# Causal attention of the first block in three steps per pair of heads instead of four, and three orders in the grid attention

## The reference

```python
# fox: bias c[t]-c[s]; causal mask; 4 blocks of 128 queries over 512 keys
logits = q @ k.T * scale + cb[:, None] - cum_logf[None, :]
p = softmax(where(kpos <= qpos, logits, -inf)); o = p @ v
# diff: two softmaxes of 32-wide queries and keys
a = softmax(mask(q1 @ k1.T * s)) - lam * softmax(mask(q2 @ k2.T * s)); o = a @ v
# dsa: the top 128 causal keys by an index score
score = sum_h w[t,h] * relu(q_idx[t,h] @ k_idx[s]); sel = top_k(where(mask, score, -inf), 128)
o = softmax(where(selected & causal, q @ k.T * scale, -inf)) @ v
```

## Time and profile before

| | us |
|---|---|
| median of three runs | 2247.26 |
| profiled execution, its own time | 2243.46 |
| its span, first to last instruction | 2241.6 |
| TensorE matmuls busy | 2187.5 |
| VectorE busy | 1257.1 |
| ScalarE busy | 899.6 |
| GpSimd busy | 288.8 |

### The profile page before, as it was taken

The page is one execution under the profiler, slowest core; times in us unless marked ns, Lnnn a source line. Parts: engine busy times, 40 slices in busy tenths (PEclk is TensorE's granted clock), DMA queues, the critical chain, the costliest instruction groups (busy, mean ns, idle before and its releaser), DMA issues.

```text
span 2241.6 us, 31809 instructions
## 1 busy us (share of the span) xinstructions
PE 2187.5 (98%) x12938; PEld 1806.5 (81%) x12938; DVE 1257.1 (56%) x1750; ACT 899.6 (40%) x1574; POOL 288.8 (13%) x215
## 2 busy tenths in 40 slices
PE   7999999999999999999999999999999999999998
PEld 6876688888888876688888888989888887888777
DVE  5687648983224687548973226422666635212794
ACT  3447843222213447843222223232565524212673
POOL 3001322111222001322121000000010000000220
PEclk9999999999999999999999999999999999999999
DMA  5220016542553220015532321132000122311221
GB/s 164 89 71 2 1 60 204 187 133 85 139 174 97 89 71 1 1 64 199 190 129 85 127 105 53 56 97 76 15 23 9 52 76 96 129 58 57 72 72 57
DMA packets 136708, 194.20 MB, mean 87 GB/s; under 512 B 30789, under 2 KB 84050, under 8 KB 136562
## 3 DMA queue, kind: packets, MB, share of 16 engines
q1 hardware_dynamic: 110288, 169.83, 22.9%
q10 hardware_dynamic: 26114, 22.16, 3.5%
q0 software_dynamic: 160, 0.16, 0.0%
HBM read 180.46 MB, written 11.67 MB: 86 GB/s over the span
## 4 chain that ended last, share of the span: by engine, by line
PE 89%; DVE 5%; ACT 2%; issue 2%; ACTq 0%; DMA 0%; POOLq 0%; POOL 0%; DVEq 0%
PE ps L530 69%; PE ps L2740 3%; PE ps L1873 3%; PE ps L2757 2%; PE ps L2769 2%; DVE probs_t L2088 1%; PE ps L2286 1%; PE ps L2243 1%; PE ps L2272 1%; PE ps L2745 1%; PE ps L737 1%; PE ps L1907 1%; ACT probs_t L2846 1%; DVE neg_max L2055 1%; PE ps L537 1%
## 5 line engine op out<-in xcount | busy, mean ns | idle before, releaser
L495 DVE TENSOR_TENSOR w_low<-w_raw,w_high 128x2048 fp32r<-128x2048 f32 (+4 forms) x140 | 302.9, 2164 | 491.5 <-ACT w_high L490 491.3
L490 ACT ACTIVATE w_high<-w_raw 128x2048 fp32r<-128x2048 f32 (+4 forms) x140 | 252.9, 1807 | 602.0 <-PE ps L530 594.3
L530 PE MATMUL ps<-h_hi,w_high 128*128 128x512 f32 (+1 forms) x1168 | 439.5, 376 | 3.1 <-DVE w_low L495 1.8
L530 PE MATMUL ps<-h_lo,w_high 128*128 128x512 f32 (+1 forms) x1168 | 437.2, 374 | 0.0
L530 PE MATMUL ps<-h_hi,w_low 128*128 128x512 f32 (+1 forms) x1168 | 436.9, 374 | 0.0
L530 PEld LDWEIGHTS ps<-h_hi,w_high 128*128 128x128 f32 x1168 | 220.0, 188 | 44.1 <-DVE w_low L495 2.4
L530 PEld LDWEIGHTS ps<-h_hi,w_low 128*128 128x128 f32 x1168 | 219.8, 188 | 39.8
L530 PEld LDWEIGHTS ps<-h_lo,w_high 128*128 128x128 f32 x1168 | 220.0, 188 | 39.2 <-issue 0.5
L530 PE MATMUL ps<-w_high,h_hi 128*128 128x512 f32 (+3 forms) x576 | 214.2, 372 | 0.6 <-DVE h_lo L3142 0.6
L530 PE MATMUL ps<-w_low,h_hi 128*128 128x512 f32 (+3 forms) x576 | 211.6, 367 | 0.0
L530 PE MATMUL ps<-w_high,h_lo 128*128 128x512 f32 (+3 forms) x576 | 211.4, 367 | 0.0
(11 more groups left out here) (388 smaller groups left out, 3704.2 us busy)
## 6 DMA issues: line engine op xcount, KB each, us to landing
w_raw<-in_w_gate_up SPq DMA_DIRECT2D x44, 1024.0 KB, 5.1
ada_w<-in_ada_w SPq DMA_DIRECT2D x24, 1024.0 KB, 5.1
w_raw<-in_w_down SPq DMA_DIRECT2D x20, 1024.0 KB, 5.2
w_raw<-in_w_in SPq DMA_DIRECT2D x16, 1024.0 KB, 5.0
w_raw<-in_c_in_w SPq DMA_DIRECT2D x16, 1024.0 KB, 5.4
w_raw<-in_w_out SPq DMA_DIRECT2D x8, 1024.0 KB, 4.8
w_raw<-in_ab_in_w SPq DMA_DIRECT2D x8, 1024.0 KB, 5.1
masked_scratch<-mask_table ACTq DMA_DIRECT2D x8, 512.0 KB, 3.5
```

The lines of the kernel that those rows point to most:

```text
L490: e.activation(w_high[j % 2][:, 0:size], w_raw[j % 2][:, 0:size], ACT.Copy).then_inc(sig.w_high_done, 1)
L495: e.tensor_tensor(w_low[j % 2][:, 0:size], w_raw[j % 2][:, 0:size], w_high[j % 2][:, 0:size].bitcast(F32), ALU.subtract).then_inc(sig.w_lo ...
L530: mm = e.matmul(dst, lhs, rhs, start=start and a == 0, stop=stop and a == 2)
```

## The change

In `CausalPairs` a unit has three steps instead of four (`TILES = ((1,), (2, 0), (3,))`): query block 1 (two key blocks), query blocks 2 and 0 side by side in the same banks (3 + 1 key blocks), query block 3 (four). There are 30 steps. In the double step there are still two reductions and four exps, but one group of transposes, one copy and one group of `values`; its block 0 gets its mask (and gate) first and q times k last. `probs_ready` now counts halves, and `turn_probs` waits for each half on its own. The 37 top-k rounds are spread over the first 23 rounds of the loop, and the first dsa unit begins with step 21. On ScalarE `copy_o(u)` now stands in the round of the next unit's second step, between `copy_probs` and `exps`. The mask of block 0 lies beside that of block 2.

In `GridPairs` `values(s - 1)` now comes ahead of `wide`, and both high halves of pair 1 are made at s = -1.

```diff
@@ CausalPairs @@
-            ROUND_STEPS = 30
-            EARLY_PARTS = {32: 0, 33: 1, 36: 2}
+            TILES = ((1,), (2, 0), (3,))
+            PER = len(TILES)
+            ROUND_STEPS = 23
+            EARLY_PARTS = {24: 0, 25: 1, 27: 2}
...
-                self.steps = [(u, t) for u in range(len(self.units)) for t in range(NT)]
+                self.steps = [(u, tiles) for u in range(len(self.units)) for tiles in self.TILES]
...
+            def parts(self, s):
+
+                at_ = 0
+                for t in self.steps[s][1]:
+                    yield t, at_, (t + 1) * P
+                    at_ += (t + 1) * P
...
                 def scores(s):
...
-                    if x.kind == "dsa" and x.n == 0 and t:
-                        e.wait_ge(sig.keep_ready, B["keep_ready"] + t)
+                    if x.kind == "dsa" and x.n == 0:
+                        e.wait_ge(sig.keep_ready, B["keep_ready"] + max(tiles))
...
+                    first = parts[-1] if len(parts) == 2 else None
+                    if first:
+                        for m in range(2):
+                            added(*first, m, True, False)
+                            if x.kind == "fox":
+                                gated(*first, m, False)
+                    for t, a, w in reversed(parts):
+                        last = first and t == 0
+                        for m in range(2):
+                            e.matmul(ps[:, self.bank(s, m), a:a + w], q[x.rows(m), t * P:t * P + P], k[x.rows(m), 0:w], start=not last, stop=bool(last))
                     for m in range(2):
-                        e.matmul(ps[:, self.bank(s, m), 0:n], q[x.rows(m), t * P:n], k[x.rows(m), 0:n], start=True, stop=False)
...
+                        mm = added(*parts[0], m, False, True)
...
                 def turn_probs(s):
-                    u, t = self.steps[s]
-                    e.wait_ge(sig.probs_ready, B["probs_ready"] + s + 1)
                     for m in range(2):
-                        for kt in range(t + 1):
...
+                        e.wait_ge(sig.probs_ready, B["probs_ready"] + 2 * s + m + 1)
+                        for b in range(self.size(s) // P):
...
                     e.wait_ge(sig.turned_second, B["turned_second"] + s + 1)
-                    if t == 0 and u:
+                    if s % self.PER == 0 and u:
                         e.wait_ge(sig.o_done, B["o_done"] + u)
...
@@ CausalPairs.scalar @@
                     if 0 <= s < self.N:
                         copy_probs(s)
+                    if s > 1 and s % self.PER == 1:
+                        copy_o(s // self.PER - 1)
                     if s in self.mid:
                         copy_turned(self.mid[s])
                     if 0 <= s + self.AHEAD < self.N:
                         exps(s + self.AHEAD)
-                    if s >= NT and s % NT == 0:
-                        copy_o(s // NT - 1)
-                    if s % NT == 2 and s > 2 and self.units[s // NT - 1].kind == "diff":
-                        shift(s // NT - 1)
+                    if s % self.PER == 2 and s > 2 and self.units[s // self.PER - 1].kind == "diff":
+                        shift(s // self.PER - 1)
...
+                copy_o(self.U - 1)
@@ GridPairs @@
-                self.cut_at = {max(4 * p - 6, -1) + c: (p, c) for p in range(1, U) for c in range(2)}
+                self.cut_at = {-1: [(1, 0), (1, 1)]}
+                self.cut_at.update({4 * p - 6 + c: [(p, c)] for p in range(2, U) for c in range(2)})
...
                         self.scores(e, B, s + 2)
+                    if s >= 1:
+                        values(s - 1)
                     if s % 4 == 3:
                         wide(s // 4)
-                    if s >= 1:
-                        values(s - 1)
```

More of the change, by code:

```diff
@@ L1094, in vector @@
                         e.wait_ge(sig.parts_ready, B["parts_ready"] + 4)
[L1095 removed]
+                        ch.step(e.tensor_copy(keep_mask[:, 2, 3 * P:4 * P], cst("causal")[:, 384:512]))
                     if i == self.groups - 1:
@@ L2703, in final, with size, both @@
             def final(self, u):
-                return NT * u + NT - 1
+                return self.PER * (u + 1) - 1
             def bank(self, s, m):
                 return 2 * (s % self.SETS) + m
-            def both(self, s, n):
+            def parts(self, s):
[3 more added lines that the diff above has]
+                    at_ += (t + 1) * P
+            def size(self, s):
+                return sum((t + 1) * P for t in self.steps[s][1])
+            def both(self, s, a, n):
                 b = self.bank(s, 0)
-                return ps[:, b:b + 2, 0:n]
+                return ps[:, b:b + 2, a:a + n]
             def spare_bank(self, e, B, event):
@@ L2738, in scores, with added @@
                     q, k = q_turned[x.group % 2], kd_turned if x.kind == "dsa" else k_turned[x.group % 2]
-                    for m in range(2):
-                        e.matmul(ps[:, self.bank(s, m), 0:n], q[x.rows(m), t * P:n], k[x.rows(m), 0:n], start=True, stop=False)
[L2741 to L2745, removed]
+                    def added(t, a, w, m, start, stop):
+                        out_ = ps[:, self.bank(s, m), a:a + w]
+                        if x.kind == "dsa":
+                            at_ = a if t == 0 else 0
+                            mm = e.matmul(out_, ident_r[:], keep_mask[:, max(tiles), at_:at_ + w], start=start, stop=stop)
+                        else:
+                            mm = e.matmul(out_[:, w - P:w], ident_r[:], causal_r, start=start, stop=stop and x.kind != "fox")
+                        return mm
@@ new lines, in gated @@
+                    def gated(t, a, w, m, stop):
+                        h = 2 * x.n + m
+                        return e.matmul(ps[:, self.bank(s, m), a:a + w], gate_sel[:, h * P:(h + 1) * P], gate_t[:, 0:w], start=False, stop=stop)
+                    first = parts[-1] if len(parts) == 2 else None
[4 more added lines that the diff above has]
+                                gated(*first, m, False)
@@ L2749, in scores @@
-                            mm = e.matmul(ps[:, self.bank(s, m), 0:n], gate_sel[:, h * P:(h + 1) * P], gate_t[:, 0:n], start=False, stop=True)
+                            mm = gated(*parts[0], m, True)
                     mm.then_inc(sig.scores_ready, 1)
                 def turn_probs(s):
-                    u, t = self.steps[s]
-                    e.wait_ge(sig.probs_ready, B["probs_ready"] + s + 1)
                     for m in range(2):
-                        for kt in range(t + 1):
-                            mm = e.transpose(ps[:, self.bank(s, m), kt * P:(kt + 1) * P],
-                                             probs1[s % 3][:, m, kt * P:(kt + 1) * P], ident)
+                        e.wait_ge(sig.probs_ready, B["probs_ready"] + 2 * s + m + 1)
@@ L2832, in exps @@
                     for m in range(2):
-                        c = 2 * s + m
-                        ins = e.activation(probs1[s % 3][:, m, 0:n], ps[:, self.bank(s, m), 0:n], ACT.Exp,
-                                           bias=neg_max[:, c:c + 1], accum_out=sums[:, c:c + 1])
-                        if m == 0:
-                            ch.step(ins)
-                    ins.then_inc(sig.probs_ready, 1)
+                        for t, a, w in self.parts(s):
+                            c = 2 * NT * u + 2 * t + m
+                            ins = e.activation(probs1[s % 3][:, m, a:a + w], ps[:, self.bank(s, m), a:a + w], ACT.Exp,
+                                               bias=neg_max[:, c:c + 1], accum_out=sums[:, c:c + 1])
+                            if t != tiles[-1]:
+                                ch.step(ins)
+                        ins.then_inc(sig.probs_ready, 1)
                 def copy_probs(s):
-                    u, t = self.steps[s]
-                    n = (t + 1) * P
+                    n = self.size(s)
                     e.wait_ge(sig.probs_turned, B["probs_turned"] + s + 1)
```

55 lines of the change are left out of this document (30 added, 25 removed).

## The result

The changed kernel takes 2286.57 us, the median of four runs: 2281.28, 2283.96, 2289.18 and a disturbed one of 8192.17, which is in no ratio but lifts the median from 2283.96. The kernel before, run beside it on the same chip, takes 2245.88: a ratio of 1.0179 (95% interval 1.0165 to 1.0193), 1.8% slower. The forecast was 2262 with a range of 2249 to 2272: the sign was right, the size was not. The profiled execution took 2283.96 us with a span of 2282.2, so against the profiled execution of before 40.5 us are to be explained, where the sum of the prediction had 15.0.

A forecast was written before the change was run, and what follows sets the result against it. TensorE was taken as the bound, with matmuls for 2187.5 of 2241.6 us. The terms -6.0 - 12.5 + 30.2 + 5.0 + 2.0 - 3.7 = +15.0 us on the median of 2247.26 gave 2262 us, range 2249 to 2272.

The forecast's parts named there:

- The standstill of `copy_o`: `values` of a unit's first step waits 1.68 us for ScalarE's late output copy, 9 units a layer: +30.2 us.
- rival 5: TensorE's clock falls in the new waits of 1.7 and 2.7 us, up to +9.8 us a unit; chance 2%.
- Waits that go, and the merge: Causal stages: one group of transposes and of `values` fewer a unit, -6.0 us; 31 waits before `scores` go, -12.5 us.
- rival 1: The merge wins: `values` does not wait for the output copy, only bank waits of about 0.5 remain; -13.2 us, 2234; chance 14%.
- the wait for the banks of step B: The double step (query blocks 2 and 0) waits for its banks; counted inside the `copy_o` standstill, no term of its own.
- The last mask: `scores(23)` of the first dsa unit waits for VectorE's last top-k mask, 2.5 us in each layer: +5.0 us.
- rival 2: VectorE paces the diff units, needing 11.2 to 12 us against TensorE's 11.5: +5 us, 2267; chance 13%.
- `shift`: In three diff units a layer ScalarE reaches the copy of step A (query block 1) 0.5 us late, delaying `scores`: +2.0 us.
- The grid attention: `wide` behind `values` saves 2.2 us, the earlier high half of the keys 1.5 net at the start: -3.7 us.
- The rule on larger operations: Skill page: break instructions up where unsaturated ScalarE causes bubbles elsewhere; by it the merge goes the wrong way; no size.

The follow-up runs named there:

- the second experiment: The kernel before with only `copy_o` moved behind `copy_probs` in the round of the next unit's second step, four steps kept: 2265.4 us, ratio 1.0103.
- the runs without rounds: The 37 top-k rounds of each causal stage left out: of the changed kernel with `copy_o` early, 2236.72 us; of the kernel before, 2244.1 us.
- the early copy: The changed kernel with `copy_o` moved back to the round of the next unit's first step, behind exps: 2250.27 us, ratio 1.0024.
- the filled standstill: The changed kernel with nine unused matmuls of 384 columns ahead of the waiting `values` in units 1 to 7 of both layers: 2275.39 us, ratio 1.0134.

## Why the prediction was right or wrong

- **The standstill of `copy_o`: right.** 1.68 us in each of 9 units was forecast, 1.69 came, 15.9 us a layer (one is 2.3) against 15.1, and its removal gives 34 us with its clock.
- **The clock: the step that failed.** The sum had 0 for it and the chance of rival 5 was 2%, on the ground of one stretch: the 2.20 us wait of the grid's start, behind which the clock had stayed at 1.00. One pause without a fall was taken as proof for 18 pauses of 1.7 us. Two traces speak against even that one. The prediction's "this trace does not show a fall" holds for that wait and not for the trace of the kernel before, which has a fall in another stage, with TensorE busy nearly all the time, behind twelve matmuls that write one column each:

```profile
1853.96 1.50 PE L3102 MATMUL ps<-ones,mod_sum 128*128 128x1 f32 x12 [0.80 <-DVE mod_sum L3067]
1855.90:1859.40 3.50, 3.40 (x14) 2.93 (x13) 1.83 (x8) 0.00 (x0) 0.00 (x0) 0.51 0.00 0
```

And the kernel of the second experiment, whose grid attention is that of before, has the same wait of 2.20 us, and there the clock falls:

```profile
2112.02 0.29 PEld L2243 LDWEIGHTS ps<-k_high,q_high 64*128 64x128 f32 x2 [2.20 <-POOL kc_low L2156]
2111.80:2115.20 3.40, 3.18 (x28) 2.93 (x28) 1.46 (x2) 0.59 (x3) 0.16 (x1) 0.50 0.34 131
```

So the stretch of the earlier trace rows was one draw of several. Measured in the changed kernel, 22 us are missing at the lower level: the largest term after the standstill itself. It isn't a fixed price of a pause either: of the nine pauses a layer, three had a fall behind them in layer 0 and six in layer 1, though eight of each nine are of 1.69 us. The mechanism of rival 5 was thus stated with its price, up to 9.8 us a unit; only its chance was wrong, and with it the range: 15 + 22 is nearly the whole of the 40.5, and without the clock the 18.5 us that are left would have been inside the range. The Trainium skill ("TensorE: Matmul & The Clock Gate", "Why this matters for your kernels") warns that idle gaps between bursts of matmuls bring the lower clock, and speaks of longer gaps than these; the trace of after, with 9 falls behind 18 pauses of 1.69 to 2.31 us, agrees in kind, and shows falls behind shorter ones.
- **Waits that go, and the merge: too large.** -6.0 - 12.5 was forecast. The old waits did go, but others came. Without rounds and without the standstill both together are worth 4.0 us, not 18.5. In the changed kernel some of the new bank waits are swallowed by the standstill (`probs_t` 0.5 us a layer against 3.0), as "the wait for the banks of step B is inside it" had it, so there the term is nearer to 2 x (2.0 + 2.5 + 1.1 + 0.9 + 0.3) = 13.6, by the differences of the two wait views. The mistake lay in rival 1, which gave the merged kernel without the standstill -13.2 us; the run of it gave +5.4. It had the bank waits (9.0, and 3.0 + 1.1 a layer are measured) but not those for `wide`, `o_raw` and `k_turned`, 1.3 + 0.9 + 0.7 a layer, which are the whole distance from 13.2 to the 7.4 of the runs without rounds, and it did not have VectorE.
- **The last mask: right in kind, 5.0 forecast, 3.7 + 2.3 = 6.0 measured.** The formula fits layer 1 (2.5 a layer against 2.3); in layer 0 the mask ran 1.1 us longer beside GpSimd.
- **VectorE as the bound (rival 2): real, but not visible in the changed kernel as such.** With the standstill in place TensorE is slow enough for it. It decides as soon as the standstill is taken away: 7 us a layer, with the clock in it. The prediction's own count, 11.2 to 12 us of VectorE against the 11.5 of TensorE, had it at the edge; with the early copy VectorE is busy 42.0 of the 48 us from 197 to 245, and 18.5 without the rounds.
- **`shift`: 2.0 forecast; open.** The waits of scores or turns for `wide` are 1.0 us a layer, where before shows none; nothing separates them from the rest.
- **The grid attention: right.** -3.7 forecast, -4.1 measured alone, -3.3 within the change; at its start 2.20 us went and 0.94 came, and of the 3.8 us before `wide` 1.4 are left.
- **The rule on larger operations** ("Perfetto Trace Analysis", "Optimizing Scalar/DVE Operations" in the Trainium skill) was weighed and then not followed to its end. The runs bear it out for this stage: ScalarE's busy time fell from 94.03 to 91.19 us a layer, where nobody needed it, and its larger pieces made TensorE wait.

The account of the 40.5 us: grid -3.3; standstill 2 x 15.9 = +31.8; mask +6.0; waits and groups saved, -13.6; clock +22; in sum +42.9, 2.4 us from what was measured. That distance is not explained; the clocks of the two stages are known to two digits, 0.7 us each.

Open too is why one pause of 1.69 us is followed by a fall and the next, of the same length and in the same place of its unit, is not; no run here separates this.

## What to carry to other kernels

A new wait of the bounding engine has two prices, its own length and the clock of what runs behind it; where the pauses recur, put the second into the sum, since one pause in the trace without a fall proves nothing about many, and one execution does not tell what the next one loses. A copy that the bounding engine needs goes ahead of work that itself waits for that engine, in the same queue: that one place in ScalarE's order was worth 34 us here, more than everything the change meant to save. And before steps are merged to save groups, check what the other engines do in the time a smaller step gave them: VectorE's 37 rounds were free in four steps and cost 7 us a layer in three.

## What was not expected of the hardware

- The granted clock fell to 0.50 with TensorE busy in nearly all of the stretch, behind pauses of 1.27 to 2.4 us, and stayed there for 3 to 10 us. It fell at every mask's wait of 3.7 to 4.0 us (five: one in the changed kernel, two each with the early copy and the filled standstill), in the shown one already before the wait had ended. The 2.28 us wait for the mask in layer 1 had none; the 2.20 us one of the earlier trace rows had none in the kernel before and one in the second experiment.
- It can fall with no pause at all near. The kernel with the grid edits alone, whose first stage is that of the kernel before, shows one fall in its profiled execution:

```profile
938.00:945.00 7.00, 7.00 (x37) 5.59 (x36) 1.94 (x5) 3.13 (x8) 0.96 (x1) 0.56 0.01 2
```

TensorE has work for all 7.00 us of it. The longest idle time of the matmuls' row in the 7 us ahead is 0.37 us, before the eight matmuls of the pair sums that write 2 columns each. This layer is 3.1 us longer for it (127.27 against 124.16 in the other), which is about the spread of this kernel's runs (2240.43 to 2243.94). The same eight matmuls in its first layer have no fall behind them. The twelve of the stage near 1855 us, which write one column each, have one in five of the ten traces. Whether such narrow outputs are a cause was not tested.
- A VectorE operation of 0.43 us took 1.50 and 1.04 us beside a GpSimd operation of 1.26 us, and 0.43 where none ran. In five masks that ran beside such an operation (changed kernel, early copy and filled standstill) the mask ended 0.28 or 0.29 us after the GpSimd operation had, whether the two began together (1.50 and 1.49 us) or GpSimd 0.51 us ahead (1.04 and 1.03). The Trainium skill ("Perfetto Trace Analysis", "Optimizing Scalar/DVE Operations") says that the two engines share a read port of SBUF; these rows fit that, but no run of its own tested it.
